# A hybrid attention and mixture-of-experts layer: where the second norm's shift is added, and which engine adds the last rows

## What is computed

```python
x = x + g1 * (mix @ w_out)
h2 = _rmsnorm(x, norm2_g) * (1.0 + sc2) + sh2
x = x + g2 * _hier_moe(h2, ...)

# _hier_moe: router, then top-1 of 4 groups, top-2 of 8 experts in it
pg = softmax(hf @ w_rg + b_rg); g_sel = argmax(pg)
le = (hf @ w_re + b_re).reshape(n, 4, 8)
pe = softmax(le[rows, g_sel]); top_w, top_i = top_k(pe, 2)
top_w = top_w / sum(top_w) * pg_sel
y = sum over the two experts of  ((silu(h @ w1) * (h @ w3)) * gate) @ w2
```

## Time and profile before

| | us |
|---|---|
| median of 3 runs | 834.54 (831.39 to 836.0) |
| the profiled execution | 838.87 |
| its span | 837.1 |
| PE busy in the span | 708.4 (85%) |
| DVE busy | 349.1 (42%) |
| ACT busy | 270.8 (32%) |
| POOL busy | 102.9 (12%) |
| expert weights, 96 loads of 1024 KB, median to landing | 24.3 |

### The profile page before, as it was taken

The page is one execution under the profiler, slowest core; times in us unless marked ns, Lnnn a source line. Parts: engine busy times, 40 slices in busy tenths (PEclk is TensorE's granted clock), DMA queues, the critical chain, the costliest instruction groups (busy, mean ns, idle before and its releaser), DMA issues.

```text
span 837.1 us, 13788 instructions
## 1 busy us (share of the span) xinstructions
PE 708.4 (85%) x5329; PEld 575.1 (69%) x5329; DVE 349.1 (42%) x549; ACT 270.8 (32%) x500; POOL 102.9 (12%) x161
## 2 busy tenths in 40 slices
PE   0798899999899999999988999737999898788760
PEld 0387788888789999999978999625565444444430
DVE  1555666666434433344323455531323232232223
ACT  0444555554353444554334541300111111011000
POOL 2012222222000000001100000010011001001023
PEclk9999999999999999999999999857999999999995
DMA  9957277665735796432315348894799999999815
GB/s 319 331 150 217 79 210 217 196 195 182 238 104 152 189 282 162 112 103 78 94 44 175 100 151 308 315 423 176 293 417 417 417 417 420 416 418 418 359 57 167
DMA packets 131176, 199.17 MB, mean 238 GB/s; under 512 B 11688, under 2 KB 113464, under 8 KB 117816
## 3 DMA queue, kind: packets, MB, share of 16 engines
q1 hardware_dynamic: 123032, 185.63, 62.7%
q0 software_dynamic: 6208, 11.02, 3.9%
q10 hardware_dynamic: 1888, 1.86, 0.7%
HBM read 193.47 MB, written 16.55 MB: 251 GB/s over the span
## 4 chain that ended last, share of the span: by engine, by line
PE 47%; DMA 16%; issue 9%; ACT 8%; DVE 8%; SPq 5%; ACTq 2%; DVEq 2%; POOLq 1%; POOL 1%
PE ps L573 22%; DMA e_w<-in_w 14%; PE ps L568 8%; PE ps L570 7%; PE ps L569 7%; ACT w_hi L1113 4%; SPq L505 3%; DVE w_lo L1426 2%; DMA vec_rows<-in_norm_g 2%; DVE w_lo L1434 1%; SPq L510 1%; ACT sig_r L1230 1%; ACT z_na L1276 1%; PE ps L990 1%; ACTq L1229 1%
## 5 line engine op out<-in xcount | busy, mean ns | idle before, releaser
L573 PE MATMUL ps<-e_w,xgT 128*64 128x256 f32 x1024 | 126.9, 406 | 29.6 <-issue 17.9
L573 PEld LDWEIGHTS ps<-e_w,xgT 128*64 128x64 f32 x1024 | 82.4, 146 | 69.8 <-issue 25.3
L568 PE MATMUL ps<-hT_hi,w_hi 128*128 128x320 f32 x320 | 102.4, 320 | 4.4 <-DVE w_lo L1426 4.2
L1426 DVE TENSOR_TENSOR w_lo<-raw,w_hi 128x2048 fp32r<-128x2048 f32 (+1 forms) x26 | 68.1, 2619 | 82.7 <-ACT w_hi L1113 82.7
L570 PE MATMUL ps<-hT_hi,w_lo 128*128 128x320 f32 x320 | 99.6, 311 | 0.0
L569 PE MATMUL ps<-hT_lo,w_hi 128*128 128x320 f32 x320 | 99.4, 311 | 0.0
L1758 DVE TENSOR_SCALAR h_s<-h_e 128x256 f32<-128x256 f32 x16 | 4.7, 294 | 157.0 <-ACT h_e L1343 157.0
L568 PEld LDWEIGHTS ps<-hT_hi,w_hi 128*128 128x128 f32 x320 | 60.8, 190 | 7.2 <-issue 4.1
L1113 ACT ACTIVATE w_hi<-raw 128x2048 fp32r<-128x2048 f32 (+1 forms) x26 | 56.4, 2168 | 21.7 <-PE ps L570 21.7
L569 PEld LDWEIGHTS ps<-hT_lo,w_hi 128*128 128x128 f32 x320 | 60.8, 190 | 0.0
L570 PEld LDWEIGHTS ps<-hT_hi,w_lo 128*128 128x128 f32 x320 | 60.7, 190 | 0.0
(11 more groups left out here) (261 smaller groups left out, 1290.4 us busy)
## 6 DMA issues: line engine op xcount, KB each, us to landing
e_w<-in_w SPq DMA_DIRECT2D x96, 1024.0 KB, 24.3
raw<-in_w_in SPq DMA_DIRECT2D x45, 512.0 KB
ada_late<-in_w_ada SPq DMA_DIRECT2D x16, 1024.0 KB, 5.2
ada_first<-in_w_ada SPq DMA_DIRECT2D x8, 1024.0 KB, 21.6
raw<-in_w_in SPq DMA_DIRECT2D x8, 1024.0 KB
raw<-in_w_oa SPq DMA_DIRECT2D x4, 1024.0 KB
raw<-in_w_ob SPq DMA_DIRECT2D x4, 1024.0 KB
raw<-in_w_out SPq DMA_DIRECT2D x4, 1024.0 KB
```

Of the source, the lines that this page charges most:

```text
L568: nc.tensor.matmul(out, lhs_hi, rhs_hi, start=first, stop=False, skip_group_check=True)
L573: return nc.tensor.matmul(out, lhs, rhs, start=first, stop=last, skip_group_check=True)
L1426: V.tensor_tensor(w_lo[j][:, :, 0:width], raw[j][:, :, 0:width], f32(w_hi[j][:, :, 0:width]), ALU.subtract).then_inc(split_done, 1)
```

## The change

Three edits in one diff.

1. A product of the router's weights with the shift columns `mod[:, 24:32]` (64 x 2) is computed on PE between the `modT` transposes and `b_iteration(1, ...)`. ACT adds `rb` and keeps it as `rbs`, one column per sequence. The router's `lgT` takes `rbs` as its bias in place of `rb`.
2. `second_rows(t)` only scales, without a drain, and signals `h2_scaled`, on which PE transposes. A new `shifted_rows(t)` adds `shift2b` in place once the tile's transposes are done (`h2_T`) and signals `h2_ready`. It runs for all three tiles behind DVE's copies of tile 2 to `xnT`, ahead of `lg`. POOL's stores and SP's wait for pair 2 stay on `h2_ready`.
3. POOL loads the result rows in the order 0, 1, 2, and DVE finishes all three tiles; POOL's three operations on tile 2 and `y_sample_done` go.

```diff
@@ -127,6 +127,7 @@
         rw_at = cursor[0]
         rw = take("rw", [P, KD, 64])
         rb = take("rb", [P, 1])
+        rbs = take("rbs", [P, 2])
         cursor[0] = max(cursor[0], rw_at + 4 * 2 * TILES * 3 * EXPERTS)
 
         x_sb = take("x_sb", [P, TILES, D])
@@ -312,7 +313,7 @@
         g2_in = sem("g2_in")
         o_done = sem("o_done"); o_added = sem("o_added")
 
-        h2_ready = sem("h2_ready"); h2_T = sem("h2_T"); h2_Ta = sem("h2_Ta"); h2_Tv = sem("h2_Tv"); h2_stored = sem("h2_stored")
+        h2_ready = sem("h2_ready"); h2_scaled = sem("h2_scaled"); h2_T = sem("h2_T"); h2_Ta = sem("h2_Ta"); h2_Tv = sem("h2_Tv"); h2_stored = sem("h2_stored")
         r_half = sem("r_half"); r_lgT = sem("r_lgT")
         r_log = sem("r_log"); r_arg = sem("r_arg"); r_exp = sem("r_exp")
         r_M = sem("r_M"); r_rows = sem("r_rows"); r_slot = sem("r_slot"); rounds_ready = sem("rounds_ready")
@@ -325,7 +326,7 @@
         e_y = sem("e_y"); e_ya = sem("e_ya"); e_yv = sem("e_yv")
         y_stored = [sem(f"y_stored{j}") for j in range(2)]
         back = [sem(f"back{t}") for t in range(TILES)]
-        y_done = sem("y_done"); y_sample_done = sem("y_sample_done"); stored = sem("stored")
+        y_done = sem("y_done"); stored = sem("stored")
 
 
         ADA_BANK = 1
@@ -551,7 +552,7 @@
             for t in range(2):
                 sp.wait_ge(y_done, t + 1)
                 sp.dma_start(t_out["y_prompt"][t * P:(t + 1) * P], x_sb[:, t, :]).then_inc(stored, 16)
-            sp.wait_ge(y_sample_done, 1)
+            sp.wait_ge(y_done, 3)
             sp.dma_start(t_out["y_sample"], x_sb[0:DEC, 2, :]).then_inc(stored, 16)
             sp.wait_ge(stored, 48)
             for s in a_stored + b_stored:
@@ -821,7 +822,7 @@
                     pe.wait_ge(b_tc_out, p)
                     if isinstance(p, int) and p == 1:
                         pe.wait_ge(b_zero, 1)
-                        pe.wait_ge(modT_out, 1)
+                        pe.wait_ge(modT_out, 2)
                     if w_on:
                         pe.wait_ge(b_w, p - 1)
                     kT, qT = b_kT[jz], b_qT[jz]
@@ -888,6 +889,10 @@
             for s in range(2):
                 last = nc.tensor.transpose(ps[0:32, 4, s * P:(s + 1) * P], mod[:, 16:48, s], ident)
             last.then_inc(modT_done, 1)
+            pe.wait_ge(router_in, 64)
+            for k in range(KD):
+                last = mm(ps[0:64, 5, 0:2], rw[:, k, :], mod[:, 24 + k, :], k == 0, k == KD - 1)
+            last.then_inc(r_half, 1)
             b_iteration(1, 1, True, True, False, False, 32)
             with pe.Fori(1, 4) as i:
                 for j in range(2):
@@ -928,7 +933,7 @@
                     out_part(u, t, range(KD)).then_inc(o_done, 1)
 
             for t in range(TILES):
-                pe.wait_ge(h2_ready, t + 1)
+                pe.wait_ge(h2_scaled, t + 1)
                 for half, b in enumerate(((0, 1), (2, 6), (7, 3))[t]):
                     for k in range(4):
                         f = (4 * half + k) * P
@@ -1288,6 +1293,8 @@
             b_iteration(0, 0, True, False, False, 48 * 9)
             act.wait_ge(modT_done, 1)
             A(modT[:], ps[0:32, 4, 0:2 * P], ACT.Copy).then_inc(modT_out, 1)
+            act.wait_ge(r_half, 1)
+            A(rbs[0:64, :], ps[0:64, 5, 0:2], ACT.Identity, bias=rb[0:64, 0:1]).then_inc(modT_out, 1)
             b_iteration(1, 1, True, True, False, 48 * 10)
             with act.Fori(1, 3) as i:
                 for j in range(2):
@@ -1318,8 +1325,8 @@
                       ACT.Copy).then_inc(h2_Ta, 1)
             act.wait_ge(router_in, 64)
             for part, sl in enumerate((slice(0, SEQ), slice(SEQ, PADDED))):
-                act.wait_ge(r_half, part + 1)
-                A(lgT[:, sl], ps[:, 4 + 2 * part, sl], ACT.Identity, bias=rb[:, 0:1]).then_inc(r_lgT, 1)
+                act.wait_ge(r_half, part + 2)
+                A(lgT[:, sl], ps[:, 4 + 2 * part, sl], ACT.Identity, bias=rbs[:, part:part + 1]).then_inc(r_lgT, 1)
             act.wait_ge(r_arg, 1)
             A(lsub[:], lsub[:], ACT.Exp).then_inc(r_exp, 1)
             act.wait_ge(r_arg, 2)
@@ -1634,8 +1641,12 @@
 
                 dve.wait_ge(late_loads, 64)
                 dve.wait_ge(n_rstd, t + 2)
-                V.scalar_tensor_tensor(h2tok[:, t, :], x_sb[:, t, :], rstd[:, t:t + 1], gain2b[:, t // 2, :], ALU.mult, ALU.mult)
-                dve.drain()
+                V.scalar_tensor_tensor(h2tok[:, t, :], x_sb[:, t, :], rstd[:, t:t + 1], gain2b[:, t // 2, :], ALU.mult,
+                                       ALU.mult).then_inc(h2_scaled, 1)
+
+            def shifted_rows(t):
+
+                dve.wait_ge(h2_T, 2 * t + 2)
                 V.tensor_tensor(h2tok[:, t, :], h2tok[:, t, :], shift2b[:, t // 2, :], ALU.add).then_inc(h2_ready, 1)
 
             for u in range(4):
@@ -1655,6 +1666,8 @@
             for half, b in enumerate((7, 3)):
                 dve.wait_ge(h2_T, 5 + half)
                 V.tensor_copy(xnT[:, 4 * half:4 * half + 4, 2 * P:3 * P], ps[:, b, :].rearrange("p (k c) -> p k c", k=4)).then_inc(h2_Tv, 1)
+            for t in range(TILES):
+                shifted_rows(t)
 
             def bc(a, n):
                 return a.unsqueeze(len(a.shape)).broadcast_to(list(a.shape) + [n])
@@ -1795,13 +1808,14 @@
 
 
             dve.wait_ge(g2_in, 16)
-            for t in range(2):
+            for t in range(TILES):
+                r = rows_of(t)
                 dve.wait_ge(back[t], 32)
-                V.tensor_tensor(ya[:, t, :], ya[:, t, :], yb[:, t, :], ALU.add)
+                V.tensor_tensor(ya[0:r, t, :], ya[0:r, t, :], yb[0:r, t, :], ALU.add)
                 dve.drain()
-                V.tensor_tensor(ya[:, t, :], ya[:, t, :], g2b[:, 0, :], ALU.mult)
+                V.tensor_tensor(ya[0:r, t, :], ya[0:r, t, :], g2b[0:r, t // 2, :], ALU.mult)
                 dve.drain()
-                V.tensor_tensor(x_sb[:, t, :], x_sb[:, t, :], ya[:, t, :], ALU.add).then_inc(y_done, 1)
+                V.tensor_tensor(x_sb[0:r, t, :], x_sb[0:r, t, :], ya[0:r, t, :], ALU.add).then_inc(y_done, 1)
 
 
         @block.gpsimd
@@ -1809,6 +1823,7 @@
             G = nc.gpsimd
             G.memset(rw[:], 0.0)
             G.memset(rb[:], 0.0)
+            G.memset(rbs[:], 0.0)
             G.memset(ones[:], 1.0)
             G.memset(ones_neg[:], -1.0)
             G.memset(eps[:], EPS)
@@ -1950,17 +1965,10 @@
             pool.wait_ge(setup_done, 1)
             for j in range(2):
                 pool.wait_ge(y_stored[j], stored_rows)
-            for t in (0, 2, 1):
+            for t in range(TILES):
                 for n, dst in enumerate((ya, yb)):
                     first, r = 1 + n * TOK + t * P, rows_of(t)
                     pool.dma_start(dst[0:r, t, :], y_dram[first:first + r]).then_inc(back[t], 16)
-            pool.wait_ge(back[2], 32)
-            pool.wait_ge(g2_in, 16)
-            G.tensor_tensor(ya[0:DEC, 2, :], ya[0:DEC, 2, :], yb[0:DEC, 2, :], ALU.add)
-            pool.drain()
-            G.tensor_tensor(ya[0:DEC, 2, :], ya[0:DEC, 2, :], g2b[0:DEC, 1, :], ALU.mult)
-            pool.drain()
-            G.tensor_tensor(x_sb[0:DEC, 2, :], x_sb[0:DEC, 2, :], ya[0:DEC, 2, :], ALU.add).then_inc(y_sample_done, 1)
 
 
 _SHAPES = (("y_prompt", (1, SEQ, D)), ("y_sample", (1, DEC, D)),
```

## The result

The changed kernel takes 837.17 us (median of 20 runs, 833.15 to 840.32) against 833.65 us for the kernel before in the same session (20 runs, 829.96 to 836.72). The ratio is 1.0041, 95% interval 1.0028 to 1.0054. The forecast was 829.5 us with a range of 827.0 to 833.0, faster. It was wrong in sign: 5.05 us were to go and 3.5 us came.

What follows compares the result with a forecast made beforehand. The bound was taken as the chain from attention through router and first gather to the expert weight stream, then the tail. Terms +0.8 - 3.1 - 2.75 = -5.05 us gave 829.5 us, range 827.0 to 833.0.

Steps and rivals of the forecast that it cites:

- The step that failed: POOL's row stores: third issued at 539.3, landing at 549, first gather due at 554.1; slack 5 us, so no cost.
- the stores come too late: First gather waits for the third store if it needs over 14.8 us, each us beyond paid in full; slower, chance 0.06.
- The 9.7 us of the prediction: Third POOL store into the running weight stream: the earlier kernel's 9.7 us was taken, so the new one lands at 549.
- The gather rival: First gather lands only when weights ahead are through, so part 2 gives nothing: -1.95 us, 832.6 us; chance 0.12.
- Part 1: Bias product on PE before b_iteration 1's Q projection: 1.0 us, net cost 0.8 us, bounds 0 to 1.85.
- Part 2 up to `lg`: Second norm and router: adds moved behind the transposes, `lg` starts at 539.3 instead of 542.78, 3.5 us sooner.
- the clock rival: Last transposes to `lg`: PE's clock falls anyway, `lg` 2.5 us sooner, total -4.05 us, 830.5 us; chance 0.15.
- Its worst case: PE at 1.2 GHz through the router, products 6 us: total -2.1 us, 832.4 us; within the rival of chance 0.15.
- Tile 2's residual: DVE in the second norm: with the add gone it ends at 530.66 instead of 531.26, 0.6 us sooner.
- I allowed 0.4 us: First gather in the full weight stream: 0.4 us lost, so 3.1 of the 3.5 us reach pair 3's issue.
- Part 3: Tail after the last weights: DVE finishes all three tiles, ending at 831.05 instead of 833.79, gain 2.75 us.
- Tile 1 does land late: Rival in the tail: tile 1 lands late, DVE stalls 1.3 us, total -3.75 us, 830.8 us; chance 0.12.

Runs made afterwards that it cites:

- experiments 1 to 4: Changed kernel without POOL's drain, 0.9976; with ACT issuing the three stores, 0.9989; kernel before plus one extra 512 KB store by POOL, 1.0042; by ACT, 0.9995.
- experiment 3: Kernel before plus one 512 KB store to scratch, issued by POOL ahead of the EV products; ratio 1.0042.
- after_interleaved: Changed kernel, drain kept, shift adds of tiles 0 and 1 placed earlier so stores go out sooner; ratio 0.9982.
- after_again: The changed kernel unaltered, timed a second time against the kernel before; ratio 1.0022.
- after_third: The changed kernel unaltered, timed a third time against the kernel before; ratio 1.0012.
- interleaved_no_drain_order: Changed kernel with shift adds placed earlier, POOL's drain removed and DVE's tail in the order 0, 2, 1; ratio 0.9953, 831.12 us.
- before_tail_order: Kernel before with DVE finishing all three tiles in the order 0, 2, 1, POOL's three operations removed; ratio 0.9939, 830.31 us.
- experiment 5: The run after_interleaved: changed kernel, drain kept, shift adds of tiles 0 and 1 placed earlier; ratio 0.9982.
- before_tail_only_2: Second timing of the kernel before plus part 3 alone (load order 0, 1, 2, DVE finishing all tiles); ratio 0.9962.

## Why the prediction was wrong, step by step

**The step that failed** is in part 2: "Behind them on POOL stand the EV products, which wait for `r_M` (about 545.5), and the gathers, which wait for the stores. [...] Slack 5 us: hidden." Between the products and the gathers stands a drain, and the runs show that it lasts until POOL's stores have landed (experiments 1 to 4). So the stores' deadline was not the gather at 554.1 but `R` at about 547.8. The second error stands beside it: the store took 13.9 us, not 9.7. Had it taken 9.7, the drain would have ended at 548.8 and cost some 0.6 us. The whole of the 4.8 us needed both.

**Third error, hidden by the first.** Without the drain the store still lands at 553.3 and the gather waits for it. The rival *the stores come too late* named this and put its threshold at 14.8 us. The gather follows the landing by 2.0 us of POOL's own steps (553.3 to 555.29), so the threshold was near 12.8, and 14.5 and 14.6 us are beyond it. That rival had the right sign and the right objects and got 0.06, since the longest store seen was 9.7 us. The sign of being wrong that the prediction gave, a first gather released by the stores, fits that run, though the trace names no releaser there.

**Why the store took longer.** Not because the weight stream was fuller: the DMA share was 1.01 and 403 GB/s flowed while the 9.7 us store was on its way (536.5 to 546.3 in the kernel before), and 1.02 and 407 GB/s during the 13.9 us. And in the same full stream (1.03) the lone extra store of experiment 3 took less:

```profile
scratch_rows<-x_sb POOLq DMA_DIRECT2D x1, 512.0 KB, 8.2
```

What the landings show is that the stores follow one another. In the changed kernel they land at 545.6, 549.3 and 553.0, in the kernel before the second and third at 542.5 and 546.3, in after_interleaved at 541.5, 545.1 and 548.8: each some 3.7 us behind the one ahead of it. The first of a row takes 7.8 to 9.4 us in the full stream. So the third store is 8.7 + 2 x 3.7 less the 2.3 us between the first and the third issue, 13.8 us. The same sum gives 9.2 + 7.4 - 5.1 = 11.5 us for after_interleaved, as measured there. The 9.7 us of the prediction was 5.9 us of waiting for the second store to land and 3.8 of its own. The change put the three adds side by side, and so the three stores, and the prediction charged only one of them. All of this is read from the landings; no run changed the distance of the stores and nothing else.

**The gather rival** (*the first gather lands only when the weights are through*) did not occur: the first gather landed 8.0 us after its issue, 8.2 before.

**Part 1: right.** 1.09 us for 16 records, where 1.0 was taken; net 0.75 us, where 0.8 was taken; 1.0 us in the mean of two timings. `rbs` on ACT was hidden as said: ACT still waits 3.46 us for the Q projection.

**Part 2 up to `lg`: right.** From Q to `lg` the kernel before takes 246.56 us. after_again and after_third take 243.07 and 243.02, 3.5 us less, the forecast's figure. The profiled execution takes 243.96, 2.6 us less, with the last transposes in 1.97 us: there the clock fell, and the clock rival's 2.5 us fits. (Its worst case, 1.2 GHz through the router, was summed as -2.1 us. Its own terms put `lg` at 533.85 + 1.97 + 6 + 1.0 = 542.8, no sooner than before, which makes -1.95.) Tile 2's residual is 0.6 us sooner, as worked out. All of it was lost behind: `lg` to gather takes 4.8 to 5.6 us more.

**Behind the gather.** I allowed 0.4 us; gather to w2 takes 37.3 us in four of the five rows above without parts 1 and 2, and 0.1 to 1.0 us more in those with them. In the changed kernel the second hidden product began at half clock, which the one of the kernel before did not; its 64 records took 8.81 us against 7.13. (The first took 9.05 against 9.73.) Windows of that product in the changed kernel:

```profile
583.80:587.20 3.40, 3.40 (x20) 2.42 (x18) 0.00 (x0) 0.00 (x0) 0.00 (x0) 0.50 1.01 422
```

and in the kernel before, at the same distance from the first hidden product:

```profile
582.96:586.36 3.40, 3.37 (x32) 2.75 (x34) 0.00 (x0) 0.18 (x1) 0.00 (x0) 1.00 1.01 422
```

The same time carries 20 records instead of 32. Why the clock differs there is not shown.

**Part 3: right in size.** 2.75 us forecast, 3.2 measured alone. Last to end is 41.10, 39.80 and 40.47 us with the old tail in the rows above and 36.9 to 38.8 with the new ones. Tile 1 does land late in half of the profiles (1.87 us of stall in the profiled execution), as that rival said, and both profiles of the order 0, 2, 1 have no such stall. The Trainium skill (SBUF — State Buffer, "Who interferes with whom") says that a DVE instruction with two SBUF inputs contends with a GpSimd instruction that reads SBUF. The trace agrees: the add takes 1.23 us with POOL idle against 1.91 beside POOL's add.

**The sum.** In single timings: part 1 +1.0, parts 1 and 2 +4.8, part 3 -3.2; together +1.6 us, beside +2.1 as the mean of three. From `modT` on the three profiles of the changed kernel give +1.8, -0.3 and +0.9 against the one of the kernel before, +0.8 in the mean. The 1.3 us between the profiles and the timings are within the spread of executions, but nothing shows where they are.

**What stays open.** interleaved_no_drain_order reaches its gather 24.0 us after `wt` where before takes 27.2, and its later stages are within 0.5 us of those of before_tail_order. From `modT` on, with the clock's 3.16 us of Q to wt (below) set aside, it should be some 2.5 us ahead of that kernel; the timings put it level or behind (0.9953 against 0.9939). So a mended part 2 has shown no gain in the timings, and where its 3 us go in the executions that were not profiled isn't known. One possible place is the clock: experiment 5 shows the same order of work with `lg` 2.9 us later. That was not shown for the median. Whether a wait for the stores' semaphores in the drain's place would do as well wasn't tried.

## What to carry to other kernels

When work is moved, look at every drain on the engines that it is moved past, and not only at the semaphores: in these runs POOL's drain was a hidden wait for the stores that POOL had in flight (loads weren't tried). Give each moved transfer two deadlines, that of its consumer and that of the next drain on its issuing engine. Count the transfers of its kind that will be in flight ahead of it, and not only how full the stream is: a duration read from spaced stores doesn't hold for stores side by side. Test a composed change by its parts: here a cheap one (the tail) was worth more than the whole.

## What the hardware showed that I had not expected

- A POOL drain of 7.9 us over 0.97 us of POOL work: 545.26 to 553.19 in the changed kernel, with its last store landed at 553.03; 7.87 us with the extra POOL store, and none with the same store from ACT.
- The time of a 512 KB store to DRAM against running weight loads: 8.7, 11.3 and 13.9 us for three issued 1.1 us apart, 3.8, 8.4 and 9.7 before; issued by ACT in the same place 14.5 for the third. A lone one in the full stream took 8.2 us from POOL and 7.8 from ACT. The issuing engine makes little difference; each store landed some 3.7 us behind the one ahead of it.
- PE's granted clock differs between executions in code that no edit touched. Windows around mix B, of the kernel before:

```profile
435.00:440.00 5.00, 5.00 (x28) 4.43 (x28) 0.00 (x0) 1.06 (x2) 0.00 (x0) 0.75 0.63 165
...
450.00:455.00 5.00, 4.69 (x21) 4.70 (x22) 4.84 (x7) 1.22 (x2) 0.00 (x0) 0.66 0.66 184
```

and of before_tail_order, which is 3.75 us ahead at `modT`:

```profile
430.00:435.00 5.00, 5.00 (x35) 4.56 (x34) 0.00 (x0) 1.19 (x2) 0.15 (x1) 1.00 0.59 147
...
445.00:450.00 5.00, 5.00 (x34) 5.00 (x35) 4.53 (x6) 0.86 (x2) 0.00 (x0) 1.00 0.73 202
```

Two falls to 1.2 GHz in one, none in the other, and 3.16 us between them in Q to wt. The profiles of before_extra_pool_dma and before_tail_only_2, with the same code up to there, have one fall and 232.5 us, halfway. That is as much as the whole effect under study: a single profiled span says nothing of a change of 3 us, a stage between two events does if its clock was the same in both.
